# Attention with two units of scores in PSUM, V turned in two portions, and the next norm's statistics on ScalarE

## The reference

```
s = einsum('bqhcd,bkhcd->bhcqk', q, k) * scale     # latent keys rotated, context keys plain
p = softmax(s)                                     # over 512 latent + 256 context keys
a = p[:, :, 0] - lam * p[:, :, 1]
out = einsum('bhqk,bkhe->bqhe', a, v)
```

## Time and profile before

| | us |
|---|---|
| median of 3 runs | 3627.74 |
| lowest, highest | 3620.80, 3630.47 |
| profiled execution, its own time | 3627.78 |
| its span, first to last instruction | 3625.8 |
| attention layer 0, about | 972 to 1171 |
| attention layer 1, about | 2863 to 3022 |

### The profile page before, as it was taken

How to read it: one execution, slowest core, us unless ns; L and a number is a source line. 1 busy time by engine, 2 the same in 40 slices (tenths; PEclk the granted TensorE clock), 3 DMA queues, 4 the chain that set the end, 5 groups by cost and what they waited for, 6 DMA issues and landing times. The chain is left out here.

```text
span 3625.8 us, 82800 instructions
## 1 busy us (share of the span) xinstructions
PE 3348.2 (92%) x36725; PEld 2699.5 (74%) x36725; DVE 1592.6 (44%) x2566; ACT 1268.9 (35%) x2188; POOL 1071.4 (30%) x645
## 2 busy tenths in 40 slices
PE   6999999999888999799999899999999898889998
PEld 4668888888755777687878676888778666668887
DVE  3243334443277656512112633445443376571224
ACT  3333233333265422321212143334344365333222
POOL 2111132233011512333333232223333113335553
PEclk8999999999999999899999999999999999999999
DMA  7663433442221443233332055344442323423332
GB/s 261 216 205 108 116 96 92 129 131 84 76 76 50 147 132 105 82 117 117 117 121 94 31 159 179 107 111 127 124 124 83 98 79 119 159 81 110 93 99 87
DMA packets 444861, 420.81 MB, mean 116 GB/s; under 512 B 15652, under 2 KB 372042, under 8 KB 437594
## 3 DMA queue, kind: packets, MB, share of 16 engines
q1 hardware_dynamic: 442922, 406.73, 35.7%
q10 hardware_dynamic: 1584, 8.78, 0.6%
HBM read 326.72 MB, written 88.74 MB: 115 GB/s over the span
## 5 line engine op out<-in xcount | busy, mean ns | idle before, releaser
L893 PE MATMUL ps<-I-321_h_hi,I-324_w_hi 128*128 128x256 f32 (+1 forms) x832 | 294.9, 354 | 4.5 <-PEq L124 4.5
L893 PE MATMUL ps<-I-322_h_lo,I-324_w_hi 128*128 128x256 f32 (+1 forms) x832 | 281.9, 339 | 0.0
L893 PE MATMUL ps<-I-321_h_hi,I-325_w_lo 128*128 128x256 f32 (+1 forms) x832 | 281.6, 338 | 0.0
L2397 POOL TENSOR_TENSOR I-18839_w_lo<-I-18837_w_raw,I-18838_w_hi 128x1024 fp32r<-128x1024 f32 x60 | 145.0, 2416 | 343.1 <-ACT I-18838_w_hi L2360 343.0
L893 PE MATMUL ps<-I-23589_h_hi,I-23592_w_hi 128*128 128x512 f32 (+1 forms) x544 | 212.2, 390 | 4.6 <-PEq L124 4.6
L893 PE MATMUL ps<-I-23590_h_lo,I-23592_w_hi 128*128 128x512 f32 (+1 forms) x544 | 200.3, 368 | 0.0
L893 PE MATMUL ps<-I-23589_h_hi,I-23593_w_lo 128*128 128x512 f32 (+1 forms) x544 | 200.2, 368 | 0.0
L2397 POOL TENSOR_TENSOR I-39098_w_lo<-I-39096_w_raw,I-39097_w_hi 128x1024 fp32r<-128x1024 f32 x60 | 144.5, 2408 | 154.6 <-ACT I-39097_w_hi L2360 154.6
L2360 ACT ACTIVATE I-18838_w_hi<-I-18837_w_raw 128x1024 fp32r<-128x1024 f32 x61 | 64.6, 1060 | 355.3 <-PE ps L370 235.3
L370 PE MATMUL ps<-I-18834_h_hi,I-18838_w_hi 128*128 128x512 f32 x704 | 182.9, 341 | 1.1 <-DVE I-18835_h_lo L407 1.1
L370 PE MATMUL ps<-I-18834_h_hi,I-18839_w_lo 128*128 128x512 f32 x704 | 181.6, 339 | 0.0
(11 more groups left out here) (904 smaller groups left out, 8743.9 us busy)
## 6 DMA issues: line engine op xcount, KB each, us to landing
I-323_w_raw<-in_w_in SPq DMA_DIRECT2D x67, 512.0 KB, 6.0
I-23591_w_raw<-in_w_in SPq DMA_DIRECT2D x67, 512.0 KB, 5.2
I-18847_ada_w<-in_ada_w SPq DMA_DIRECT2D x24, 1024.0 KB, 5.9
I-18837_w_raw<-in_ffn_up SPq DMA_DIRECT2D x44, 512.0 KB, 3.8
I-39096_w_raw<-in_ffn_up SPq DMA_DIRECT2D x44, 512.0 KB, 3.8
proj_d<-I-1999_result SPq DMA_DIRECT2D x52, 384.0 KB, 3.1
I-507_ada_w<-in_ada_w SPq DMA_DIRECT2D x16, 1024.0 KB, 5.6
I-18837_w_raw<-in_ffn_down SPq DMA_DIRECT2D x22, 512.0 KB, 3.3
```

Of the source, the lines that this page charges most:

```text
L893: m = pe.matmul(bank(6 + i % 2, n_c), w[:, k, :], hv[:, k, c0:c0 + n_c], start=k == 0 and v == 0, stop=k == KT - 1 and v == 2)
L2397: pool.tensor_tensor(pair(g)[1], rings[0][:, g % 3, :, :], pair(g)[0].bitcast(F32), ALU.subtract).then_inc(sem("w_lo"), 1)
```

## The change

Four things. (1) A unit's two score sets lie together in three banks: latent scores of c = 0 in the first, both context parts in the second, latent scores of c = 1 in the third. The two sets of banks hold two units. For c = 1 the keys are in another order (context first, the latent halves swapped), so that one reduction over a regular view gives both maxima; the exponential reads the thirds backwards. (2) The streams are reordered: `scores(n+2)`, then a portion of V, then `values(n-1)`, then `turn(n)`; o is copied by ScalarE. (3) V of the next head is turned in two portions, four tiles at u = 1 and two at u = 2, both into bank 6. (4) `next_stats` goes to ScalarE: a copy with a running sum, a scaling to the negative mean, a square of the difference with a running sum. `norm` starts from these; the setup stage derives them from its bn_stats.

```diff
@@ norm @@
-                for t in range(nt):
-                    i = dve.bn_aggr(mv[:, t, :], st_x[:, t, :, :])
-                i.then_inc(sem("n_mv"), 1)
-                dve.wait_ge(sem("n_mv"), 1)
-                dve.tensor_scalar(rs[:, 0:nt], mv[:, 0:nt, 1], LN_EPS, None, ALU.add).then_inc(sem("n_var"), 1)
+                dve.tensor_scalar(rs[:, 0:nt], x_ss[:, 0:nt], 1.0 / D_MODEL, LN_EPS, ALU.mult, ALU.add).then_inc(sem("n_var"), 1)
...
@@ attention @@
-            score = lambda n, c, w, o=0: ps[:, ((2 * n + c) % 3) * 1024 + o:((2 * n + c) % 3) * 1024 + o + w]
+            near = lambda n: (n % 2) * 3 * 512
+            ctx_at = lambda n, c: near(n) + (SEQ + c * CTX_LEN if units[n][1] < LT else CTX_LEN + c * TOK)
+            near_ctx = lambda n, c: ps[:, ctx_at(n, c):ctx_at(n, c) + CTX_LEN]
+            near_lat = lambda n, c: ps[:, near(n) + 2 * c * SEQ:near(n) + (2 * c + 1) * SEQ]
+            thirds = lambda ap: ap.rearrange("p (a b) -> p a b", b=CTX_LEN)
...
-                            sp.wait_ge(sem("s1_mm"), (j - 1) * nq)
-                            sp.wait_ge(sem("v_mm"), j - 1)
+                            sp.wait_ge(sem("s_mm"), (j - 1) * nq)
+                            sp.wait_ge(sem("v_mm"), 2 * (j - 1))
...
+                        if n >= 2:
+                            pe.wait_ge(sem("exp"), 2 * (n - 1))
...
+                        if u < LT:
+                            lat(0)
+                            ctx(1).then_inc(sem("ctx1"), 1)
+                            lat(1)
+                            pe.wait_ge(sem("ctx1"), j * LT + u + 1)
+                            m = ctx(0)
+                        else:
+                            ctx(0)
+                            m = ctx(1)
+                        m.then_inc(sem("s_mm"), 1)
...
                     for n, (j, u) in enumerate(units):
-                        if n + 1 < N:
-                            pe.wait_ge(sem("exp0"), n + 1)
-                            pe.wait_ge(sem("exp1"), n + 1)
-                            scores(((n + 1, 1), (n + 2, 0)) if n + 2 < N else ((n + 1, 1),))
+                        if n + 2 < N:
+                            scores(n + 2)
+                        if u in (1, 2) and j + 1 < HA:
+                            v_turn(j + 1, u - 1, n)
+                            n_v += 1
                         if n:
-                            values(n - 1, n_v)
+                            values(n - 1)
                         turn(n, n_v)
-                        if u == 1 and j + 1 < HA:
-                            v_turn(j + 1, n + 1)
-                            n_v += 1
...
@@ attention, scalar @@
+                    def o_copy(n):
+                        act.wait_ge(sem("o"), n + 1)
+                        act.activation(oq[:, n, :], o_ps, ACT.Copy).then_inc(sem("o_read"), 1)
...
                         if n + 1 < N:
-                            soft(n + 1, 1)
+                            soft(n + 1)
+                        if u in (1, 2) and j + 1 < HA:
+                            v_copy(j + 1, u - 1)
+                        if n:
+                            o_copy(n - 1)
                         act.wait_ge(sem("aT_mm"), n + 1)
...
@@ attention, vector @@
+                        dve.tensor_reduce(mx[:, n % 3, :], both_scores(n), AX.X, ALU.max, negate=True).then_inc(sem("max"), 1)
...
                     for n, (j, u) in enumerate(units):
+                        if n + 1 < N:
+                            maximum(n + 1)
                         combine(n)
-                        if n + 1 < N:
-                            maximum(n + 1, 1)
-                        if n:
-                            o_copy(n - 1)
-                        if n + 2 < N:
-                            maximum(n + 2, 0)
...
@@ close, scalar (ffn of layer 0 the same) @@
+                    def next_stats(t):
+                        act.wait_ge(sem("xb"), t + 1)
+                        act.activation(unread[t % 2], x[:, t, :], ACT.Copy, accum_out=x_nm[:, t:t + 1]).then_inc(sem("x_sum"), 1)
+                        act.wait_ge(sem("x_sum"), t + 1)
+                        act.activation(x_nm[:, t:t + 1], x_nm[:, t:t + 1], ACT.Copy, scale=-1.0 / D_MODEL).then_inc(sem("x_nm"), 1)
+                        act.wait_ge(sem("x_nm"), t + 1)
+                        act.activation(unread[t % 2], x[:, t, :], ACT.Square, bias=x_nm[:, t:t + 1], accum_out=x_ss[:, t:t + 1])
+
                     for t in range(nt):
                         root(t)
+                        next_stats(t)
...
@@ close, vector @@
-                        next_stats(t)
```

More of the change, by code:

```diff
@@ L1424, in ready, with scores, lat, ctx @@
                             pe.wait_ge(sem(f"q_in{j % 2}"), 16 * (j // 2 + 1))
[L1426 to L1430, removed]
-                        half = lambda c: slice(c * DH_A, (c + 1) * DH_A)
[L1432 to L1440, removed]
+                    def scores(n):
+                        j, u = units[n]
+                        ready(n)
+                        if n >= 2:
+                            pe.wait_ge(sem("exp"), 2 * (n - 1))
+                        half = lambda c: slice(c * DH_A, (c + 1) * DH_A)
+                        def lat(c):
+                            k = thirds(kr[half(c), j % 2, :])
+                            return pe.matmul(thirds(near_lat(n, c)), qr[half(c), j % 2, u * P:(u + 1) * P], k if c == 0 else k[:, ::-1, :],
+                                             start=True, stop=True)
+                        def ctx(c):
+                            return pe.matmul(near_ctx(n, c), qp[half(c), j % 2, u * P:(u + 1) * P], kp[half(c), j % 2, :], start=True, stop=True)
+                        if u < LT:
[8 more added lines that the diff above has]
+                        m.then_inc(sem("s_mm"), 1)
                     def turn(n, n_v):
@@ L1489, in soft, with v_copy @@
-                    def soft(n, c):
+                    def v_copy(j, part):
+                        ts = v_part[part]
+                        o = 0 if j else ts[0] * P
+                        act.wait_ge(sem("v_mm"), 2 * j + part + 1)
+                        act.activation(vt[:, j % 2, ts[0]:ts[-1] + 1, :].rearrange("p t d -> p (t d)"), aT_ps(o, o + len(ts) * P),
+                                       ACT.Copy).then_inc(sem("vt"), 1)
+                    def soft(n):
                         w = n_keys(units[n][1])
-                        if n >= 3 and c == 0:
+                        if n >= 3:
@@ L1492, in soft @@
                             act.wait_ge(sem("aT_mm"), n - 2)
[L1493 to L1500, removed]
+                        act.wait_ge(sem("max"), n + 1)
@@ L1501, in _ @@
+                    soft(0)
+                    v_copy(0, 0)
+                    v_copy(0, 1)
                     for n, (j, u) in enumerate(units):
@@ L1530, in _, with maximum @@
                 def _(dve):
[L1531 to L1536, removed]
+                    def maximum(n):
+                        if n >= 3:
+                            dve.wait_ge(sem("exp"), 2 * (n - 2))
+                        dve.wait_ge(sem("s_mm"), n + 1)
+                        dve.tensor_reduce(mx[:, n % 3, :], both_scores(n), AX.X, ALU.max, negate=True).then_inc(sem("max"), 1)
                     def combine(n):
                         w = n_keys(units[n][1])
-                        dve.wait_ge(sem("exp0"), n + 1)
-                        dve.wait_ge(sem("exp1"), n + 1)
+                        dve.wait_ge(sem("exp"), 2 * n + 2)
                         dve.reciprocal(rec[:, n % 3:n % 3 + 1], sm[:, n, 1:2]).then_inc(sem("rec"), 1)
@@ L2256, in pair @@
                     return [v[:, :, :].rearrange("p k n -> p (k n)")[:, e * KT * P:(e + 1) * KT * P].rearrange("p (a b) -> p a b", a=KT) for v in h]
+                unread = [v[:, :, :].rearrange("p k n -> p (k n)")[:, 6 * TOK:6 * TOK + D_MODEL] for v in hp] if not last else None
                 tap = lambda i, j: pb[l][:, PB["conv"] + i * FT + j:PB["conv"] + i * FT + j + 1]
@@ L2488, in _ @@
                             scaled(t)
-                            if not last:
-                                next_stats(t)
         for l in range(DEPTH):
```

95 lines of the change are left out of this document (55 added, 40 removed).

## The result

| | median of the runs, us | ratio to the kernel before (95% interval) |
|---|---|---|
| before | 3629.1 (3620.8 to 3635.1, 4 runs) | |
| after | 3593.4 (3584.0 to 3595.2, 4 runs) | 0.9900 (0.9876 to 0.9923) |
| forecast | 3577 (3556 to 3604) | |

The account below looks back on a forecast made before the run. TensorE, busy 92% of the span, was taken as the bound, with VectorE bounding the norms' ends. Gains 18 + 23.5 + 10 - 1 = 50.5 us, from 3627.8, gave 3577 us, range 3556 to 3604.

Parts of the forecast that it names:

- the narrower 3565 to 3590: Whole kernel: the band in us around the forecast time of 3577, given a chance of 0.60.
- Strided reads are dear: Rival, attention: reading the second map in thirds backwards runs at half speed, giving 3592 us; chance 0.08.
- attention, layer 0: Layer 0's attention stage: a head falls from 23.95 to 20.85 us, stalls included; 23.5 us gained in all.
- attention, layer 1: Layer 1's attention stage: a head falls from 18.70 to 16.3 us, wait before V gone; 18 us gained in all.
- three norm ends: Layer 0's close, layer 1's close, layer 0's ffn: statistics leave VectorE, gaining 4.9, 2.5 and 2.5, together 10 us.
- setup: Setup stage: added aggregations (0.57 us) and two small operations after a wait, taken as wholly exposed; 1 us lost.
- The matmul order: Attention scores on TensorE: lat(0), ctx(1), lat(1), wait, ctx(0) was taken to cost 1.49 us, as the old order did.
- Program order holds the halves: Rival, attention scores: unlike widths run in strict order, 1.91 us, 0.42 more on 64 units, giving 3604 us; chance 0.10.
- the hand schedule: One layer 0 attention head followed: stalls of 0.6, 0.3, 0.6 and 0.4 us, 1.9 a head.
- no table load between Sqrt and Square: ScalarE in the norm ends: Square needs no table switch, so nothing added; the contrary reading would cost 7.7 us.
- the end of layer 0's ffn: Norm end there: last tile starts 3.4 us earlier, limited by TensorE's end; 2.5 us gained.
- The slower rival: Rival, attention: the four score matmuls don't overlap, 1.27 us more on 64 units, giving 3658 us; chance 0.03.

Follow-up runs that it names:

- Experiments 1 to 3: Changed kernel with score passes reordered: ctx(1) issued first, 3571.8 us; context pair issued last, 3619.6 us; lat(0) cut in two pieces around ctx(1), 3572.2 us.
- experiment 3: Changed kernel with lat(0) cut into two 256-column passes, one issued ahead of ctx(1) and one behind it: 3572.2 us, ratio 0.9851.
- experiment 1: Changed kernel with ctx(1) issued ahead of lat(0) in each full unit, wait and passes kept: 3571.8 us, ratio 0.9841; repeats 3581.4 and 3577.0 us.

## Why the prediction was right, and what its sum had wrong

The time came out within the range and 16 us above the forecast. That it lies within is owed to the width that the range was given for rivals which did not come true: it is outside the narrower 3565 to 3590 that the forecast itself stood for, and the case nearest to it, "Strided reads are dear" (3592), is out. Three errors partly cancel in it: the order of the score matmuls costs 17.5 us, some 9 are lost in other stages, and the rest of attention gained about 10 more than forecast. In this table the stages are taken in the profiled executions, from the first score matmul to the end of the last square sum:

| | before | forecast gain | after (gain) | ctx(1) first (gain) |
|---|---|---|---|---|
| attention, layer 0 | 199.7 | 23.5 | 179.9 (19.8) | 171.8 (27.9) |
| attention, layer 1 | 159.0 | 18 | 145.2 (13.8) | 135.8 (23.2) |
| three norm ends | | 10 | (9.7) | |
| setup | | -1 | (-0.3) | |

**The step that was mis-sized is "The matmul order": "I take 1.49 again".** It is 1.83 in the new order, and putting it right gives 8.1 + 9.4 = 17.5 us, 0.27 on each of the 64 full units (0.33 in an undisturbed one; other waits, layer 0's above all, take the rest). In medians it is 18 us (3593.4 to 3575.5). Why the rows of before did not show it: at the head boundary of the earlier trace rows unlike widths do run side by side, but no instruction there stands waiting for the short matmul's signal. The overlap of the work was carried over rightly; the release of its signal was not priced. The trace of before had it all the same, in its semaphore increments. The 256-column matmul that starts at 1063.59 ends by the model at 1064.29, and its increment comes at 1065.19, 0.06 us after the end of the one issued ahead of it (1065.13).

**The rival "Program order holds the halves"** had the right kind of cause at the wrong place. It let the other half start late and gave 1.91; the halves start 0.01 us apart (2950.02 and 2950.03), and it is the signal that is held. The Trainium skill, "TensorE: Matmul & The Clock Gate", section "The mechanism", states order for the ends of matmuls too, and draws from it that a signal on the last matmul vouches for all before it. Experiments 1 to 3 agree as to signals; what follows for a signal in the middle is its other side, 0.46 us of waiting here. The order of starts, which the prediction took from there for this rival, does not hold across the halves: in the earlier trace rows the matmul that starts at 1063.59 is the last issued of its group, 0.95 us ahead of the start (1064.54) of the one issued before it in the other half.

**The rest of attention was forecast too low.** With the order mended both stages gain 51.1 us where I had summed 41.5. A head of layer 1 takes 16.05 us (forecast 16.3), one of layer 0 20.76 (forecast 20.85); and the granted clock of layer 1's stage, 0.94 before, is 0.98 after, for which I had allowed little. Before, that stage ran its first 12.5 us and two stretches of 3.4 at the lower level, layer 0's its first 12.7; with ctx(1) first it is 4.2 and 2.8. Half of the difference, some 12 us, is the most that this can have given (an estimate, as if all work there took twice as long).

These are the rows of both attention stages, layer 1 first, before and then after (the mean granted clock, of levels 2.4 and 1.2 GHz, is the third number from the end):

```profile
2863.40:3022.40 159.00, 140.98 (x880) 96.78 (x880) 116.50 (x200) 93.35 (x170) 17.43 (x34) 0.94 0.23 72
972.20:1171.90 199.70, 168.81 (x1040) 114.68 (x1040) 147.71 (x296) 115.62 (x250) 23.84 (x50) 0.97 0.19 62
```

```profile
2841.10:2986.30 145.20, 140.32 (x880) 100.78 (x880) 110.02 (x136) 99.26 (x210) 20.11 (x34) 0.98 0.24 78
972.50:1152.40 179.90, 168.16 (x1040) 117.61 (x1040) 134.18 (x200) 122.81 (x306) 26.81 (x50) 0.98 0.21 69
```

**Some is given back elsewhere.** The stages touched gain 43 us in the traces, the span 33.6. Two stretches lose 10 us together and so hold the missing 9, first layer 1's stages from the norm up to its attention, then the merge and close behind it; before, then after:

```profile
2083.60:2863.38 779.78, 728.99 (x13064) 599.98 (x13065) 330.79 (x570) 294.30 (x577) 236.98 (x139) 0.98 0.42 124
3022.40:3240.80 218.40, 184.06 (x740) 139.20 (x740) 133.45 (x179) 78.50 (x112) 81.47 (x46) 0.95 0.42 137
```

```profile
2054.90:2841.06 786.16, 729.46 (x13064) 598.51 (x13065) 333.11 (x570) 293.98 (x577) 236.93 (x139) 0.98 0.40 123
2986.30:3205.40 219.10, 187.29 (x740) 142.66 (x740) 127.72 (x167) 89.01 (x132) 82.26 (x46) 0.93 0.42 136
```

The first is 6.4 us longer. It took 775 to 790 us over the profiles of these kernels, whichever part of the change they have (785.2 with attention alone, 789.6 with the norm part alone, 775.0 in experiment 3), so nothing ties it to the change; with one profile of each that is all that can be said. The second should be 2.95 shorter and is 0.7 longer, 3.6 lost. It is 215.8 with the norm part alone and 222.0 with attention alone, so this loss goes with the attention change; its clock is lower, 0.93 for 0.95. Whether the denser attention ahead of it brings the lower clock was not tried and stays open.

**Point by point.** Right: both exponentials of 768 columns 0.90 us and the maximum 1.76 (forecast 1.75), so "Strided reads are dear" is out; o's copy on ScalarE 0.28 (0.3); no wait for exponentials and none ahead of V in layer 1; the waits of layer 0's units behind short scores at the places that the hand schedule had (0.67, 0.47 and 0.67 us for 0.3, 0.6 and 0.4); the norm ends, and no table load between Sqrt and Square. Wrong beside the order and the sizes above: the setup, where the aggregations cost 0.3 and not 1, and the end of layer 0's ffn, which gained 1.7 and not 2.5. The slower rival is out: the halves do overlap, and the wait costs nothing once it is met early (experiment 1).

## What to carry to other kernels

When an instruction waits for a matmul in the middle of a group, count the time to the end of everything issued before that matmul, in the other half of the rows too; so issue first the one that is waited for. A matmul pattern copied from a place where nobody waits for it gives the price of the work, not of its signal. And a stage whose TensorE shows 100% busy can still hold stalls: the brackets on its weight loads name them.

## What was not expected of the hardware

Two halves of TensorE's rows start 0.01 us apart, yet the shorter matmul's signal came 1.19 us after its start when a 512-column matmul was issued ahead of it, within 0.76 behind one of 256 columns, and 0.65 where all before it ended first. The halves need not even start in the order of issue: at the earlier trace rows the matmul issued last starts 0.95 us before the one ahead of it. Reading PSUM in thirds backwards cost ScalarE nothing (0.90 us for 768 columns either way); VectorE reads it forwards, 1.76 us for both maps' 1536 columns.
